# Gathering an expert's token rows in turned form: residual rows stationary, one-hots moving

## What is computed

```
logits = xt @ w_router + b_router                # 256 x 32
top_val, top_idx = top_k(logits, 4); gate = softmax(top_val)
for each expert e, for the tokens x_e that chose it:
    hdn = x_e @ w_mlp1[e] + b_mlp1[e]            # 1024 -> 2048
    glu = min(hdn[:, :1024], 7); lin = clip(hdn[:, 1024:], -7, 7)
    act = glu * sigmoid(1.702 * glu) * (lin + 1)
    y_e = act @ w_mlp2[e] + b_mlp2[e]            # 1024 -> 1024
h += sum of gate * y_e over a token's experts; out = rmsnorm(h)
```

## Time and profile before

| | |
|---|---|
| median of three runs | 1120.61 us |
| profiled execution, its own time | 1120.70 us |
| its span | 1118.7 us |
| PE busy | 1081.9 us (97%) |
| DVE / ACT busy | 368.2 us (33%) / 246.9 us (22%) |
| weights and all else read | 437.67 MB, 392 GB/s over the span |

### The profile page before, as it was taken

One profiled execution on the slowest core, in us unless ns is written; L12 is line 12 of the kernel. 1 busy time (PEld: TensorE's weight loads), 2 busy tenths in 40 slices (PEclk: granted clock), 3 DMA queues, 4 the chain that ended last, 5 costly groups with the idle time before them and its releaser, 6 DMA issues.

```text
span 1118.7 us, 14432 instructions
## 1 busy us (share of the span) xinstructions
PE 1081.9 (97%) x5393; PEld 485.3 (43%) x5394; DVE 368.2 (33%) x813; ACT 246.9 (22%) x346; POOL 3.0 (0%) x12
## 2 busy tenths in 40 slices
PE   9999999999999999999999999999999999999996
PEld 8888888533333333333333333333333333333332
DVE  6987786422222122222222222222222222222223
ACT  6745674311111111111111111111111111111112
POOL 0000000000000000000000000000000000000000
PEclk9999999999999999999999999999999999999999
DMA  9654479999999999999999999999999999999996
GB/s 337 230 186 152 151 221 421 427 412 427 428 428 435 431 429 432 433 430 432 432 431 396 431 431 432 433 433 433 431 431 431 433 431 431 431 431 431 424 424 277
DMA packets 38165, 439.15 MB, mean 393 GB/s; under 512 B 5276, under 2 KB 5464, under 8 KB 22424
## 3 DMA queue, kind: packets, MB, share of 16 engines
q1 hardware_dynamic: 37776, 437.78, 93.5%
q10 hardware_dynamic: 360, 0.95, 0.3%
HBM read 437.67 MB, written 1.05 MB: 392 GB/s over the span
## 4 chain that ended last, share of the span: by engine, by line
PE 80%; DMA 13%; DVE 6%; issue 1%; SPq 0%; ACT 0%; DVEq 0%; PEldq 0%
PE bank L1161 35%; PE bank L1190 18%; DMA ring<-in_w_mlp_dram 11%; PE bank L806 9%; PE bank L1088 3%; PE bank L1172 2%; PE bank L800 2%; DMA late_slots<-in_w_mlp_dram 2%; PE bank L968 2%; PE bank L1016 2%; DVE xn L1678 2%; DVE xn L1675 2%; DVE xn L1682 2%; PE bank L1064 1%; PE bank L1072 1%; PE bank L1138 1%
## 5 line engine op out<-in xcount | busy, mean ns | idle before, releaser
L1161 PE MATMUL bank<-ring,xn 128*64 128x512 f32 x1232 | 276.3, 595 | 6.3 <-DMA ring<-in_w_mlp_dram 6.3
L1161 PE MATMUL bank<-late_slots,xn 128*64 128x512 f32 x880 | 197.3, 595 | 3.6 <-DMA late_slots<-in_w_mlp_dram 3.5
L1161 PEld LDWEIGHTS bank<-ring,xn 128*64 128x64 f32 x1232 | 84.6, 136 | 163.6 <-issue 150.1
L1190 PE MATMUL bank<-ring,smo 128*64 128x512 f32 x624 | 138.3, 595 | 0.0
L713 ACT ACTIVATE xn<-bank 128x512 f32<-128x512 f32 x33 | 19.8, 599 | 479.9 <-PE bank L1161 479.9
L1161 PEld LDWEIGHTS bank<-late_slots,xn 128*64 128x64 f32 x880 | 60.4, 136 | 116.1 <-issue 106.5
L1691 DVE SCALAR_TENSOR_TENSOR moe_y_lo<-bank,st,moe_y_hi 128x512 fp32r<-128x512 f32 x33 | 24.8, 751 | 235.9 <-ACT moe_y_hi L720 235.9
L1675 DVE TENSOR_SCALAR xn<-bank 128x512 f32<-128x512 f32 x33 | 22.8, 692 | 219.4 <-PE bank L1161 219.4
L1190 PE MATMUL bank<-late_slots,smo 128*64 128x512 f32 x416 | 92.4, 595 | 0.2 <-DMA late_slots<-in_w_mlp_dram 0.2
L1190 PEld LDWEIGHTS bank<-ring,smo 128*64 128x64 f32 x624 | 43.0, 137 | 81.0 <-issue 81.0
L720 ACT ACTIVATE moe_y_hi<-bank,st 128x512 fp32r<-128x512 f32 x33 | 22.7, 687 | 234.1 <-PE bank L1190 234.1
(11 more groups left out here) (271 smaller groups left out, 886.3 us busy)
## 6 DMA issues: line engine op xcount, KB each, us to landing
ring<-in_w_mlp_dram SPq DMA_DIRECT2D x43, 4096.0 KB, 30.2
late_slots<-in_w_mlp_dram SPq DMA_DIRECT2D x29, 4096.0 KB, 27.8
ring<-in_w_mlp_dram SPq DMA_DIRECT2D x28, 2048.0 KB, 13.2
late_slots<-in_w_mlp_dram SPq DMA_DIRECT2D x15, 2048.0 KB, 15.3
ring<-in_w_in_dram SPq DMA_DIRECT2D x22, 1024.0 KB, 5.6
late_slots<-in_w_mlp_dram SPq DMA_DIRECT2D x6, 1024.0 KB, 35.9
ring<-in_w_branch_dram SPq DMA_DIRECT2D x4, 1024.0 KB, 5.0
ring<-in_w_out_dram SPq DMA_DIRECT2D x4, 1024.0 KB, 7.3
```

Source lines behind the costliest of these rows:

```text
L1161: last = mm(B[4 + u][g * C:(g + 1) * C, :], xgT[:, k % 4, k // 4, :], by_group(held[k // 2][0][:, k % 2, u * FF:(u + 1) * FF], g), start=F ...
L1190: last = mm(B[7][g * C:(g + 1) * C, :], actT[:, j, h * C:(h + 1) * C], held[4 + h][0][:, j // 2, (j % 2) * D + g * N:(j % 2) * D + (g + 1) ...
```

## The change

The operands of the gather's matmuls change places. The residual rows become stationary: for each half `t` of the tokens, each `j` of 4 and each `g` of 2 a block of 128 columns of `xs`, taken with a step of four elements (columns j, j+4, j+8, ... of half `g`). The one-hots move, 64 columns. The result is 128 features by 64 places, at once in the turned form that `take_xgT` expects. ACT's copy `take_xg`, PE's `turn_rows` and the buffer `xg` go; `take_xgT` waits for the gather itself.

```diff
-            def take_xg(ready):
-                act.wait_ge(gath, ready)
-                nc.scalar.activation(xg.rearrange("p (s q) -> p s q", s=ROWS),
-                                     B[6][:, :].rearrange("p (q s) -> p s q", s=ROWS), ACT.Copy).then_inc(xg_out, 1)
-
-            take_xg(1)
...
-                take_xg(i + 2)
...
                 for t in range(TT):
                     pe.wait_ge(onehot, ready - 1 + t)
-                    for g in range(2):
-                        last = mm(B[6][g * C:(g + 1) * C, :], oneh[:, t, :], xs[:, t, g * N:(g + 1) * N],
-                                  start=(t == 0), stop=(t == TT - 1), skip_group_check=True)
+                    for j in range(ROWS):
+                        for g in range(2):
+                            rows_of = xs[:, t, g * N:(g + 1) * N].rearrange("p (q s) -> p s q", s=ROWS)[:, j, :]
+                            last = mm(B[6][:, (2 * j + g) * C:(2 * j + g + 1) * C], rows_of, oneh[:, t, :],
+                                      start=(t == 0 and j == 0 and g == 0), stop=(t == TT - 1), skip_group_check=True)
                 last.then_inc(gath, 1)
...
-            def turn_rows(ready):
-
-                pe.wait_ge(xg_out, ready)
-                for j in range(4):
-                    last = nc.tensor.transpose(B[6][:, j * P:(j + 1) * P], xg[:, j * P:(j + 1) * P], ident)
-                last.then_inc(xg_turned, 1)
...
-            turn_rows(1)
...
-                turn_rows(i + 2)
...
             def take_xgT(ready):
-                dve.wait_ge(xg_turned, ready)
+                dve.wait_ge(gath, ready)
```

More of the change, by code:

```diff
@@ L249, in build @@
         xgT = moe[:, 0:N].rearrange("p (j g s) -> p j g s", j=4, g=2)
-        xg = moe[:, N:2 * N]
         lin = moe[:, 2 * N:3 * N]
@@ L304, in build @@
         row_ready, biased = sem("bias_row_ready"), sem("biased")
-        onehot, gath, xg_out, xg_turned, xg_ready = (sem("onehot"), sem("gathered"), sem("xg_out"), sem("xg_turned"),
-                                                      sem("xg_ready"))
+        onehot, gath, xg_ready = sem("onehot"), sem("gathered"), sem("xg_ready")
         gated_ready, gt_turned, gT_ready = sem("gated_ready"), sem("gates_turned"), sem("gatedT_ready")
```

## The result

The changed kernel takes **1355.69 us**, the median of four runs (1354.93 to 1356.25), against 1120.78 us for the kernel before, run beside it (four runs, 1120.59 to 1121.72). The ratio is 1.2093 with a 95% interval of 1.2078 to 1.2108: 21% slower, where 1142.3 us and at most 1197 had been forecast. The sign was right and the size was wrong by a factor of eleven.

The account below looks back on a forecast made before the run. PE and DMA both looked full, PE having 11.7 us of slack against the weight stream. On PE's path 33 x 1.0 + 0.3 - 11.7 = 21.6 us, added to 1118.7 and 2.0 around it: 1142.3 us, range 1133 to 1197.

Parts of the forecast that it names:

- The rule for the end: The kernel's end moves by the larger of 33d + f - 11.7 (PE) and 14d + f (DMA): 21.6 us.
- d: How much longer one item takes on PE, from gather to second weights: forecast 1.0 us.
- f: How much longer the first gather, which stands alone, takes up to the first weights: forecast 0.3 us.
- What the removed parts give back: Between gather and second weights: of the four transposes' 0.60 us, 0.3 comes back; ACT's copy is worth nothing.
- the hole: At the 15th item DMA has nothing to do for 2.4 us; a faster PE would win only that.
- 32 plain loads at 110 ns, matmul under the load, the first one 0.07 us before the end of `L1161`: Each item's gather: 32 weight loads hiding their 64-column matmuls, 3.52 us, starting at about 524.92.
- I take the load as unhindered, 110 ns: In the gather, weight loads with a step of four elements were taken to cost no more than contiguous ones.
- stepped loads at half pace: Rival for the gather: each load waits one more load time, 220 ns apart, d = 4.5, 1261 us; chance 0.14.
- No term below is a clock term: Whole kernel: PE's granted clock is full throughout before the change, so the forecast gave the clock no cost.
- DMA only waits for PE afterwards: After the change PE's path is the longer, 21.6 against 14.3 us; the chain is nearly without DMA steps.
- slack: PE's spare time over the whole kernel before the change, as it was faster than the weight stream: 11.7 us.

Follow-up runs that it names:

- two of the experiments: Changed kernel gathering 128 neighbouring columns, without the step: 1144.80 us; kernel before with a step of four in its moving rows, ACT's copy plain: 1159.76 us.
- doubled gather: Changed kernel with neighbouring columns in the gather and every gather matmul issued twice, 64 loads an item: 1293.43 us.

## Why the prediction was wrong, point by point

- **The rule for the end** (33d + f - 11.7 on PE's path): right, also in two of the experiments (24.1 for 24.5, 39.5 for 39.2). With the measured d = 7.30 and f = 4.3 (the first `L1146` load at 216.85, not 212.59) it gives 33 x 7.30 + 4.3 - 11.7 = 233.5 us; the span grew by 1353.9 - 1118.7 = 235.2. The lower clock falls on the first item's first weights too, behind the first gather, which no term of the rule holds.
- **What the removed parts give back** (-0.3): right, -0.29 without the turns. That the hole would close by 2.4 us was too much: 1.7.
- **32 plain loads at 110 ns, matmul under the load, the first one 0.07 us before the end of `L1161`**: right. Neighbouring columns: 112 ns, d = 1.05, 1144.8 us, where 1142.3 was the forecast. The first gather's f was 1.2 there, where 0.3 was summed from estimated hops. The number forecast is in effect that of the change without its step.
- **"I take the load as unhindered, 110 ns": the step that failed.** It measures 233. I had priced a stepped read of SBUF by PE's weight load with ACT's stepped read of a PSUM bank (`L701`), another engine on another memory, because its rate per element was near. The stretched row on DVE (`L1682`) spoke for a price, and got less weight. The rival "stepped loads at half pace" (0.14) had nearly the size, 220 ns and d = 4.5; its reason, one more load time for each, is not what steps two and three show (118 and 174 ns). The step's own part is 33 x 3.93 = 130 us of the 235; 32 x (0.233 - 0.112) = 3.87 us says nearly the same.
- The Trainium skill, "SBUF — State Buffer", section "Door 1: The DMA port swizzle", was cited against the forecast: 16-byte lines, of which at least two hits are needed. The runs agree on both points: step two (two hits) is 118 ns against 112, step four (one hit) 233, step eight (still one) 237. It would have been right to follow it, as far as to the rival's 1261 us. The same passage of the page gives 4 fp32 elements as the distance that can be strided for free; taken as a step of four elements, that is not so here, where a step of four makes a load 2.1 times as dear.
- **"No term below is a clock term": failed too**, and no rival had it. The earlier trace rows show a full clock for the old gather's 512-column matmuls; that says nothing of a gather that moves 64 columns every 233 ns. Size: 2.32 us an item, 33 x 2.32 = 77 us, a third of the loss. With 112 ns a load it did not come (clock 0.997), so it hangs on the failed step; but the rival at half pace, 1261 us, is 95 us too low, mostly by it.
- **DMA only waits for PE afterwards**: right; the chain is PE throughout.

In sum: 35 us form (33 x 1.05), 130 us step, 77 us clock, 4 us first gather, less 11.7 of slack, is 234 of 235 us.

Shown by runs: that the step, not the form, doubles the loads' distance; that the distance goes with the 16-byte pieces; that with denser matmuls in the same gather the clock stays up. What the chip does inside to make a piece cost 1.82 ns, and the exact condition of the clock's fall, are not shown: with the split gather and with step three some of the items were slow and some not. The doubled gather's clock fell only at PE's stops.

## What to carry to other kernels

The operand that is made stationary should lie in memory as neighbouring elements, or at least two to every 16 bytes; a step that is free on one engine's read of a bank has to be priced by a row of the same engine on the same memory, and where there is none, the rival with the price deserves as much as the one without. Where a swap of operands turns few wide matmuls into many narrow ones behind slow loads, ask for the clock as well: what lies behind them pays. And price a saving by what it gives back on the engine that bounds; here copy and turns were worth 0.3 us of an item of 27, so little could be won by any form of this change.

## What the runs showed of the hardware

- **Stepped weight loads.** A load of 128 columns in float32 follows another after 112 ns for neighbouring columns, and after 1.82 ns for each 16-byte piece touched where that is more (118 ns for 64 pieces, 174 for 96, 233 for 128, 237 for 128 at a step of eight). For step four it is the same at either level of the clock, 232 and 233 ns.
- **Stepped moving operands.** A pair of 512-column MATMULs takes 0.43 us without a step, 0.45 with a step of two, 0.89 with four; the last two are 0.87 ns for each piece.
- **The clock falls with PE busy.** From 2.4 to 1.2 GHz in a gather of 64 columns every 233 ns, PE at 4.00 of 4.00 us in both windows of the gather; some 4 us of the second weights ran at the lower level, 12 MATMULs where 22 were done after. With 64 columns every 174 ns (step three) the second weights were slowed in 30 of 33 items, with the gather in two bursts of 3.9 us in 23 of 33; 64 every 112 ns, or 128 every 233, did not bring the clock down.
- **Stops at the loop's end.** One wait of the gather for both one-hots, in place of two, made PE stop four times for 9.1 to 10.4 us, with 60 instruction packets instead of 24, 48 us in all on the time: a difference of some per cent between two kernels need not come from the edit that was made.
